# The lower part of the query times the upper part of the key, as two 64-row matmuls in two halves of the array

## Chip, cores and metric

The kernel runs on one core of a Trainium2 chip. The metric is the device time of one execution in microseconds (us). TensorE is called PE in the profile, its weight loads PEld, VectorE is DVE, ScalarE is ACT, GpSimd is POOL, and SP is the engine whose queue issues the DMAs here.

## The reference

One layer of a decoder: a normed input is projected to queries, keys and values of 8 heads of 64 and to a gated short convolution; then an output projection and a SwiGLU feed-forward part. The change lies in the attention scores, the line with `z` below.

```python
def one_block(args):                      # 128 queries of every head
    z = jnp.einsum('bhqd,bhkd->bhqk', q_blk, k32) * scale
    causal = key_pos[None, :] < q_pos[:, None]
    sp = jax.nn.softplus(z)
    neg_log_rem = jnp.where(causal, sp, 0.0)
    after = lax.cumsum(neg_log_rem, axis=3, reverse=True) - neg_log_rem
    a = jnp.where(causal, jnp.exp((z - sp) - after), 0.0)
    return jnp.einsum('bhqk,bhkd->bhqd', a, v32)
```

The sequence has 2048 tokens, so a head has 16 query blocks (t = 0 to 15) of 128 and, for block t, t + 1 key blocks of 128.

## The kernel before, in words

Numbers are kept as a rounded upper part and the rest as a lower part, both in the type fp32r. The program has an opening (projection to q, k, v), the attention stage with the convolution's projections woven in, the output projection and the feed-forward part. The attention stage loops over 4 pairs of heads; in a pair it runs 48 units, 24 for each head. A unit is one query block t against up to 8 key blocks (`SB`), that is up to 1024 keys, and these fill one or two PSUM banks of 512 columns. A head has 16 units with two banks: 10 with 8 key blocks and 2 each with 7, 6 and 5; so all 8 heads have 128, with a second bank of 512 columns in 80, of 384 in 16, of 256 in 16 and of 128 in 16.

`scores` computes a unit on PE. In `k_st` the upper part of 64 key rows lies on partitions 0 to 63 and the lower part on 64 to 127. `q_hh` holds the upper part of the query on both halves, `q_ll` the lower part on both. So one matmul over 128 rows gives upper query times (upper + lower key) (line 1347), and a second gives lower query times (upper + lower key) (line 1348). A unit on the diagonal adds the causal mask by a bf16 matmul with the identity (line 1351). The last matmul of a unit raises `z_full`; then ACT makes two sigmoids of the scores (lines 1107, 1109), DVE scans their running product (line 1210, `scan_done`) and POOL multiplies (line 1269, `a_done`). `scores` of unit n waits for the scan of unit n-2, since `z` has two buffers.

The order on PE is written out by hand in `body`: scores of unit n, then a number of steps of the convolution's projection (`project_step`, lines 107 to 109, counts in the table `plan`), the transposes of unit n-3 (line 1363) and, at the end of a group, the products with the values (lines 1369, 1370). Each matmul is preceded by its own weight load, which overlaps matmuls before it.

The keys come in by `load_k` (line 959) and `load_k_rest` (line 965), on SP's queue. It is also this queue that issues the loads of the queries (line 976), of the projection's inputs `hT` (line 991) and weights (line 997), of the values (line 981) and the stores.

Of the kernel before, what the change touches and what calls it, by code (L numbers as in the profile page):

```python
# [20 lines left out]
F32 = mybir.dt.float32  # L21
# [6 lines left out]
P = 128  # L28
BANK = 512
EPS = 1e-6  # L30
MASKED = -1e30
DMA = 16


def wait(eng, sem, value):

    if not isinstance(value, int) or value > 0:
        eng.wait_ge(sem, value)
# [166 lines left out]
def whole_layer(nc, cst, x, norm_mix, w_in, q_norm, k_norm, conv_w, w_out, norm_ffn, w_gate, w_up, w_down, out, HD,  # L205
                hT_hi_dram, hT_lo_dram, qk_hi_dram, qk_lo_dram, v_dram, mixT_dram, wt_dram, x2_dram, h2_dram, ops_dram):

    with ExitStack() as stack:
# [40 lines left out]
        opening = qkv_stage(nc, stack, cst, qkv, ps, x, norm_mix, w_in, q_norm, k_norm, w_down, hT_hi_dram, hT_lo_dram,  # L249
                            qk_hi_dram, qk_lo_dram, v_dram, wt_dram)  # L250
        att_stage = attend_conv_stage(nc, stack, cst, att, ps, opening, hT_hi_dram, hT_lo_dram, w_in, conv_w, qk_hi_dram,
                                      qk_lo_dram, v_dram, mixT_dram, HD)

# [576 lines left out]
def attend_conv_stage(nc, stack, cst, sb, ps, opening, hT_hi_dram, hT_lo_dram, w_in, conv_w, qk_hi_dram, qk_lo_dram, v_dram,  # L830
                      mixT_dram, HD):

    D, S = hT_hi_dram.shape
# [9 lines left out]
    QB = 4  # L843
# [5 lines left out]
    CT = CD // P  # L849
    NPROJ = 3 * CT  # L850
    HALO = TAPS - 1
    COL0 = w_in.shape[1] - 3 * CD
    assert S // BANK == PAIRS and NG % QB == 0

# [4 lines left out]
    for gi, (h, g) in enumerate(groups):  # L859
        for i in range(GT):  # L860
            t = GT * g + i
# [49 lines left out]
    def is_first(p):  # L911

        return isinstance(p, int) and p == 0
# [5 lines left out]
    with ExitStack():  # L919
        m = Pool_(nc, stack, "att_")  # L920
        k_st, q_hh, q_ll, v_st, stick, a, aT_hi, aT_lo, o_low, o_sb, hT_hi, hT_lo, w_stage, w_hi, w_lo = (
            sb[n] for n in ("k_st", "q_hh", "q_ll", "v_st", "stick", "a", "aT_hi", "aT_lo", "o_low", "o_sb",
                            "hT_hi", "hT_lo", "w_stage", "w_hi", "w_lo"))
        taps, halo, c_sb, cu, conv, tapped, y = (
            sb[n] for n in ("taps", "halo", "c_sb", "cu", "conv", "tapped", "y"))
        z = [ps[:, 4 * i:4 * i + 2, :].rearrange("p b c -> p (b c)") for i in range(2)]
        tr = ps[:, 2:4, :].rearrange("p b (j t) -> p b j t", t=P)
        o, proj = ps[:, 7, :], ps[:, 6, :]
        TILES, SAFE = opening.tiles, opening.tiles - 3

        k_in, v_in = [m.sem("k_in0"), m.sem("k_in1")], [m.sem("v_in0"), m.sem("v_in1")]
# [21 lines left out]
        def sync(sp, mix):  # L953
            def load_k(p, h):
                wait(sp, z_full, NU * (p - 1) + head_end[h])
                rows = bass.ds((2 * p + h) * HD + AD, HD)
                keys = slice(0, SAFE * P if is_first(p) and h == 0 else S)
                for half, src in enumerate((qk_hi_dram, qk_lo_dram)):
                    sp.dma_start(k_st[half * HD:(half + 1) * HD, h, keys].bitcast(F32),
                                 src[rows, keys]).then_inc(k_in[h], DMA)  # L960

            def load_k_rest():

                for half, src in enumerate((qk_hi_dram, qk_lo_dram)):
                    sp.dma_start(k_st[half * HD:(half + 1) * HD, 0, SAFE * P:S].bitcast(F32),
                                 src[AD:AD + HD, SAFE * P:S]).then_inc(k_rest, DMA)

            def load_q(p, gi):
# [25 lines left out]
            def load_w(p, k):  # L994
                wait(sp, w_lo_done, NPROJ * p + k - 1)
                col = COL0 + (1, 2, 0)[k % 3] * CD + (k // 3) * P
                sp.dma_start(w_stage[:, k % 2, :, :], w_in.rearrange("(k p) f -> p k f", p=P)
# [22 lines left out]
            def load_ahead(sp):  # L1020

                load_w(0, 0)
                load_w(0, 1)
                sp.wait_ge(opening.qkT_stored[0], 2 * DMA * (SAFE // 2 + 1))
                sp.wait_ge(opening.qkT_stored[1], 2 * DMA * (SAFE // 2))
                sp.wait_ge(opening.xn_done, TILES)
                sp.wait_ge(opening.ss_done, TILES)
                load_k(0, 0)
                for gi in range(QB):
                    load_q(0, gi)  # L1030
# [9 lines left out]
            def start_up():  # L1040
                for b in range(2):
                    sp.wait_ge(opening.v_stored[b], DMA * TILES // 2)
                    sp.wait_ge(opening.qkT_stored[b], DMA * TILES)
                    sp.wait_ge(opening.hT_stored[b], DMA * TILES)
                load_v(0, 0)
                load_k_rest()
# [3 lines left out]
            def body(p):  # L1050
                if is_first(p):
                    start_up()
                for n, (gi, h, t, j0, nb) in enumerate(units):
# [11 lines left out]
                    if n == 9:  # L1065
                        load_k(p, 1)
# [15 lines left out]
                    if not is_last(p):  # L1082
                        if n == head_end[0] + 2:
                            load_k(p + 1, 0)
                        if n == head_end[0] + LAG + 3:
                            load_v(p + 1, 0)
                        for i in plan.reloads.get(n, ()):
                            load_hT(p + 1, i)
# [12 lines left out]
        def scalar(act, mix):  # L1101
# [27 lines left out]
            def take(p, k):  # L1129
                c = k // 3  # L1130
                if k % 3 == 1:
                    wait(act, conv_done, CT * p + c)
                    wait(act, halo_moved, 2 * (CT * p + c))
                    if is_first(p) and c == 0:
                        act.wait_ge(edges_set, 2)
                    nc.scalar.activation(cu[:, 0:HALO], halo[:, c, :], ACT.Copy).then_inc(halo_moved, 1)
                act.wait_ge(proj_full, NPROJ * p + k + 1)
# [7 lines left out]
                elif k % 3 == 1:  # L1145
                    nc.scalar.activation(cu[:, HALO:HALO + BANK], proj, ACT.Copy).then_inc(proj_out, 1)
                else:
                    wait(act, y_stored, DMA * (CT * p + c))
                    nc.scalar.activation(y[:, :], proj, ACT.Copy).then_inc(proj_out, 1)
                    act.wait_ge(cu_done, CT * p + c + 1)  # L1150
                    nc.scalar.activation(halo[:, c, :], cu[:, BANK:BANK + HALO], ACT.Copy).then_inc(halo_moved, 1)

# [110 lines left out]
        def gpsimd(pool, mix):  # L1263
# [8 lines left out]
            def c_times_u(p, c):  # L1272
                pool.wait_ge(proj_out, NPROJ * p + 3 * c + 2)
                nc.gpsimd.tensor_tensor(cu[:, HALO:HALO + BANK], cu[:, HALO:HALO + BANK], c_sb[:, :],
                                        ALU.mult).then_inc(cu_done, 1)
# [53 lines left out]
        def tensor(pe, mix):  # L1329
            def scores(p, n):  # L1330
                gi, h, t, j0, nb = units[n]
                if opens[n]:
                    if gi % HG == 0:
                        pe.wait_ge(k_in[h], 2 * DMA * p + 2 * DMA)
                    pe.wait_ge(q_in[gi % QB], 4 * DMA * (NG // QB) * p + 4 * DMA * (gi // QB + 1))
                if is_first(p) and h == 0 and t == SAFE:
                    pe.wait_ge(k_rest, 2 * DMA)
                if is_first(p) and n == 1:
                    pe.wait_ge(opening.qk_n_done, 2 * TILES)
                    pe.wait_ge(opening.v_done, TILES)  # L1340
                wait(pe, scan_done, NU * p + n - 1)
                tile = slice((t % GT) * P, (t % GT + 1) * P)
                for b0 in range(0, nb * P, BANK):
                    b1 = min(nb * P, b0 + BANK)
                    diagonal = j0 + b1 // P == t + 1
                    out, keys = z[n % 2][:, b0:b1], slice(j0 * P + b0, j0 * P + b1)
                    nc.tensor.matmul(out, q_hh[:, gi % QB, tile], k_st[:, h, keys], start=True, stop=False)  # L1347
                    last = nc.tensor.matmul(out, q_ll[:, gi % QB, tile], k_st[:, h, keys],  # L1348
                                            start=False, stop=not diagonal)
                    if diagonal:  # L1350
                        last = nc.tensor.matmul(z[n % 2][:, b1 - P:b1], cst["ident_bf"][:, :], cst["mask_bf"][:, :],  # L1351
                                                start=False, stop=True)
                last.then_inc(z_full, 1)

            def transposes(p, n):
# [60 lines left out]
            def body(p):  # L1416
                for n in range(NU):
                    scores(p, n)
                    if is_first(p) and n == 0:
                        rest(0)  # L1420
                        rest(1)
                    for k, i in plan.steps[n]:
                        project_step(p, k, i)
                    q, b = at(p, n - LAG)
                    closes = opens[b] and (n > LAG or not is_first(p))
                    if closes:
                        upper_values(q, units[b][0] - 1)
                    if n >= LAG or not is_first(p):
                        transposes(p, n - LAG)
                    if closes:  # L1430
                        lower_values(q, units[b][0] - 1)
                    for k, i in plan.held[n]:
                        project_step(p, k, i)
# [14 lines left out]
        p, half = PAIRS - 1, DMA * NG // 2  # L1448
# [1200 lines left out]
```

## Time and profile before

| what | value |
|---|---|
| median of 3 runs | 2471.56 us (2466.45 to 2473.23) |
| the profiled execution's own time | 2467.11 us |
| its span, first to last instruction | 2465.3 us |
| PE busy in the span | 2423.8 us, 98%, 12008 matmuls |
| weight loads busy | 2023.1 us, 82% |
| DVE, ACT, POOL busy | 59%, 47%, 50% |
| chain of work that ended last | 92% on PE |

Busy time of an engine is the time in which at least one of its instructions runs. Matmuls overlap: one of 512 columns is shown with some 390 ns, while the next begins 0.23 us after it. So a matmul's cost to the program is read from the distance between two starts in the timeline, not from its own length.

### The profile page before, as it was taken

The page shows a single profiled execution, that of the slowest core. Times are in us where ns is not written, and L with a number is a line of the kernel's source. Part 1 is how long each engine was busy: PE and PEld are TensorE (multiplying, and loading weights), DVE is VectorE, ACT ScalarE, POOL GpSimd, SP SyncE. Part 2 cuts the span into 40 slices and gives each one's busy share as a digit, 9 for nine tenths or more (in the row PEclk, how much of TensorE's full clock was granted, in tenths as well). Part 3 has the DMA queues.
Part 4 walks back from the last instruction along what each step waited for, and adds up shares of the span by engine and source line. Part 5 has one row for each costly group of instructions (what it writes and reads, how often), then busy time and mean ns, then how long its engine had stood idle before and what let it go on. Part 6 is the DMA issues. An engine that isn't in the chain of part 4 may idle for free.

```text
span 2465.3 us, 34564 instructions
## 1 busy us (share of the span) xinstructions
PE 2423.8 (98%) x12008; PEld 2023.1 (82%) x12008; DVE 1456.8 (59%) x1499; ACT 1167.8 (47%) x1866; POOL 1238.5 (50%) x882
## 2 busy tenths in 40 slices
PE   8999999999999999999999999999999999999999
PEld 6888878888888888888788888878878888888887
DVE  4444367787677777536665555456646555554554
ACT  4322267777777777423533333334533333333333
POOL 1455366878777777204654545305856545450021
PEclk9999999999999999999999999999999999999999
DMA  6989864443534632444333232486642332325665
GB/s 196 319 285 291 255 183 122 140 114 100 164 95 114 175 112 75 153 135 164 124 115 111 87 122 82 144 269 232 226 165 80 112 128 77 115 94 184 222 216 201
DMA packets 337513, 388.15 MB, mean 157 GB/s; under 512 B 21473, under 2 KB 242785, under 8 KB 335073
## 3 DMA queue, kind: packets, MB, share of 16 engines
q1 hardware_dynamic: 337376, 386.49, 49.7%
q8 instruction: 67, 1.10, 0.2%
q14 instruction: 70, 0.57, 0.1%
HBM read 263.20 MB, written 123.21 MB: 157 GB/s over the span
## 4 chain that ended last, share of the span: by engine, by line
PE 92%; DVE 2%; DMA 2%; issue 1%; ACT 1%; POOL 1%; SPq 0%; ACTq 0%; DVEq 0%; POOLq 0%
PE lay_ps L2549 11%; PE lay_ps L2551 11%; PE lay_ps L2553 11%; PE lay_ps L107 9%; PE lay_ps L108 9%; PE lay_ps L109 9%; PE lay_ps L2579 5%; PE lay_ps L2581 5%; PE lay_ps L2580 5%; PE lay_ps L1363 5%; PE lay_ps L1347 3%; PE lay_ps L1348 3%; PE lay_ps L1370 3%; PE lay_ps L1369 2%; DMA lay_A_over<-in_w_down 1%
## 5 line engine op out<-in xcount | busy, mean ns | idle before, releaser
L2453 POOL TENSOR_TENSOR lay_A<-lay_raw,lay_A 128x512 fp32r<-128x512 f32 x264 | 364.9, 1394 | 384.9 <-ACT lay_A L2079 384.9
L2549 PE MATMUL lay_ps<-lay_B,lay_A 128*128 128x512 f32 x1232 | 481.0, 390 | 3.6 <-ACT lay_s L2101 3.6
L2551 PE MATMUL lay_ps<-lay_B,lay_A 128*128 128x512 f32 x1232 | 480.7, 390 | 0.0
L2553 PE MATMUL lay_ps<-lay_B,lay_A 128*128 128x512 f32 x1232 | 480.6, 390 | 0.0
L1210 DVE TENSOR_TENSOR_SCAN lay_stick<-lay_ps,lay_stick 128x128 f32<-128x128 f32 (+5 forms) x192 | 331.1, 1725 | 140.4 <-ACT lay_ps L1109 138.3
L1269 POOL TENSOR_TENSOR lay_a<-lay_a,lay_stick 128x128 f32<-128x128 f32 (+5 forms) x192 | 281.6, 1473 | 120.5 <-DVE lay_stick L1210 107.9
L2326 DVE TENSOR_TENSOR lay_A<-lay_A_over,lay_A 128x1024 fp32r<-128x1024 f32 x154 | 212.6, 1383 | 173.7 <-ACT lay_A L2123 173.1
L2079 ACT ACTIVATE lay_A<-lay_raw 128x512 fp32r<-128x512 f32 x264 | 162.1, 627 | 298.3 <-DMA lay_raw<-in_w_gate 124.5
L2123 ACT ACTIVATE lay_A<-lay_A_over 128x1024 fp32r<-128x1024 f32 x154 | 163.1, 1060 | 243.6 <-PE lay_ps L2581 201.2
L2549 PEld LDWEIGHTS lay_ps<-lay_B,lay_A 128*128 128x128 f32 x1232 | 232.0, 188 | 52.7 <-issue 2.6
L2553 PEld LDWEIGHTS lay_ps<-lay_B,lay_A 128*128 128x128 f32 x1232 | 232.0, 188 | 48.4
L2551 PEld LDWEIGHTS lay_ps<-lay_B,lay_A 128*128 128x128 f32 x1232 | 232.0, 188 | 48.0
L2579 PE MATMUL lay_ps<-lay_A 128*128 128x512 f32 x616 | 240.6, 391 | 3.9 <-ACT lay_s L2134 1.4
L2580 PE MATMUL lay_ps<-lay_A 128*128 128x512 f32 x616 | 239.7, 389 | 0.0
L2581 PE MATMUL lay_ps<-lay_A 128*128 128x512 f32 x616 | 239.7, 389 | 0.0
L1222 DVE TENSOR_TENSOR lay_aT_lo<-lay_ps,lay_aT_hi 128x512 fp32r<-128x512 f32 (+2 forms) x320 | 179.7, 594 | 24.7 <-ACT lay_aT_hi L1120 24.2
L1120 ACT ACTIVATE lay_aT_hi<-lay_ps 128x512 fp32r<-128x512 f32 (+2 forms) x320 | 156.2, 532 | 50.6 <-PE lay_ps L1363 50.3
L1107 ACT ACTIVATE lay_a<-lay_ps 128x128 f32<-128x128 f32 (+5 forms) x192 | 149.5, 779 | 64.7 <-PE lay_ps L1351 35.9
L107 PE MATMUL lay_ps<-lay_hT_hi,lay_w_hi 128*128 128x512 f32 x384 | 164.9, 429 | 3.2 <-issue 3.2
L2296 DVE TENSOR_TENSOR lay_s<-lay_ps,lay_s 128x512 f32<-128x512 f32 x132 | 90.2, 688 | 130.6 <-PE lay_ps L2553 92.9
L1363 PE MATMUL lay_ps<-all_ident,lay_a 128*128 128x128 f32 x1088 | 153.1, 275 | 6.3 <-DVE lay_aT_lo L1222 5.9
L2101 ACT ACTIVATE lay_s<-lay_ps 128x512 f32<-128x512 f32 x132 | 78.1, 592 | 166.2 <-PE lay_ps L2553 163.4
(148 smaller groups left out, 4954.4 us busy)
## 6 DMA issues: line engine op xcount, KB each, us to landing
hid_ops<-lay_s SPq DMA_DIRECT2D x154, 256.0 KB, 2.1
lay_A_over<-hid_ops SPq DMA_DIRECT2D x154, 256.0 KB, 2.8
lay_w_stage<-in_w_in SPq DMA_DIRECT2D x48, 512.0 KB, 4.7
lay_raw<-in_w_gate SPq DMA_DIRECT2D x22, 1024.0 KB, 5.7
lay_raw<-in_w_up SPq DMA_DIRECT2D x22, 1024.0 KB, 8.1
lay_A_over<-wd_ops SPq DMA_DIRECT2D x88, 256.0 KB, 3.0
lay_A_over<-in_w_down SPq DMA_DIRECT2D x66, 256.0 KB, 4.5
lay_wd_raw<-in_w_down SPq DMA_DIRECT2D x11, 1024.0 KB, 6.7
```

What stands on the lines that cost most here:

```text
L107: nc.tensor.matmul(out, lhs_hi, rhs_hi, start=first, stop=False)
L108: nc.tensor.matmul(out, lhs_hi, rhs_lo, start=False, stop=False)
L1210: nc.vector.tensor_tensor_scan(stick[:, row % 2, c0:c1][:, ::-1], z[n % 2][:, 0:nb * P][:, ::-1], stick[:, row % 2, S:S + 1].to_broadcast( ...
L1269: nc.gpsimd.tensor_tensor(a[:, n % 4, 0:nb * P], a[:, n % 4, 0:nb * P], stick[:, row_of[n] % 2, c0:c0 + nb * P], ALU.mult).then_inc(a_done, 1)
L1363: last = nc.tensor.transpose(tr[:, f % 2, i, :], a[:, n % 4, (j + i) * P:(j + i + 1) * P], cst["ident"][:, :])
L2453: nc.gpsimd.tensor_tensor(A[:, j, p, 1, :, :], operand(j, p), A[:, j, p, 0, :, :].bitcast(F32), ALU.subtract).then_inc(lo_done, 1)
L2549: nc.tensor.matmul(ps[:, b, :], A[:, j, p, 0, k, :], B[p][:, 0, k, :], start=first_mm, stop=False, skip_group_check=True)
L2551: nc.tensor.matmul(ps[:, b, :], A[:, j, p, 0, k, :], B[p][:, 1, k, :], start=False, stop=False, skip_group_check=True)
L2553: mm = nc.tensor.matmul(ps[:, b, :], A[:, j, p, 1, k, :], B[p][:, 0, k, :], start=False, stop=last_mm, skip_group_check=True)
L2579: nc.tensor.matmul(to, hi_op[:, toks], hi_op[:, wd_part], start=first, stop=False, skip_group_check=True)
L2580: nc.tensor.matmul(to, hi_op[:, toks], lo_op[:, wd_part], start=False, stop=False, skip_group_check=True)
L2581: mm = nc.tensor.matmul(to, lo_op[:, toks], hi_op[:, wd_part], start=False, stop=c == ROUNDS - 1, skip_group_check=True)
```

## The change

In a unit with two banks the upper-query matmuls of both banks now come first. Then the lower-query matmuls follow, and each has only 64 rows: for the first bank rows 0 to 63, for the second rows 64 to 127. In every second block of 512 keys the upper part of the key lies on partitions 64 to 127 and the lower part on 0 to 63, so that each 64-row matmul reads the upper part of its keys. The product of lower query and lower key is left out in these units. Units with one bank keep the 128-row matmul. The mask comes after all of these. The two 64-row matmuls of a unit are built for an array of 64 by 128 at row 0 and at row 64; all others use the whole 128 by 128. The loads of the keys are cut at every 512 keys: 8 DMAs for a head where there were 2.

```diff
+    KEY_LOADS = 2 * S // BANK
...
-                keys = slice(0, SAFE * P if is_first(p) and h == 0 else S)
+                end = SAFE * P if is_first(p) and h == 0 else S
                 for half, src in enumerate((qk_hi_dram, qk_lo_dram)):
-                    sp.dma_start(k_st[half * HD:(half + 1) * HD, h, keys].bitcast(F32),
-                                 src[rows, keys]).then_inc(k_in[h], DMA)
+                    for b in range(0, S, BANK):
+                        place = (half + b // BANK) % 2 * HD
+                        keys = slice(b, min(b + BANK, end))
+                        sp.dma_start(k_st[place:place + HD, h, keys].bitcast(F32), src[rows, keys]).then_inc(k_in[h], DMA)
...
-                for b0 in range(0, nb * P, BANK):
+                banks = range(0, nb * P, BANK)
+                for b0 in banks:
                     b1 = min(nb * P, b0 + BANK)
-                    diagonal = j0 + b1 // P == t + 1
                     out, keys = z[n % 2][:, b0:b1], slice(j0 * P + b0, j0 * P + b1)
                     nc.tensor.matmul(out, q_hh[:, gi % QB, tile], k_st[:, h, keys], start=True, stop=False)
-                    last = nc.tensor.matmul(out, q_ll[:, gi % QB, tile], k_st[:, h, keys],
-                                            start=False, stop=not diagonal)
-                    if diagonal:
-                        last = nc.tensor.matmul(z[n % 2][:, b1 - P:b1], cst["ident_bf"][:, :], cst["mask_bf"][:, :],
-                                                start=False, stop=True)
+                diagonal = j0 + nb == t + 1
+                for b0 in banks:
+                    b1 = min(nb * P, b0 + BANK)
+                    out, keys = z[n % 2][:, b0:b1], slice(j0 * P + b0, j0 * P + b1)
+                    half = slice(0, P) if len(banks) == 1 else slice(HD * (b0 // BANK), HD * (b0 // BANK) + HD)
+                    last = nc.tensor.matmul(out, q_ll[half, gi % QB, tile], k_st[half, h, keys],
+                                            start=False, stop=not diagonal or b0 != banks[-1])
+                if diagonal:
+                    last = nc.tensor.matmul(z[n % 2][:, (nb - 1) * P:nb * P], cst["ident_bf"][:, :], cst["mask_bf"][:, :],
+                                            start=False, stop=True)
                 last.then_inc(z_full, 1)
```

The first place is on PE, in the first head pair: a unit with 7 key blocks (banks of 512 and 384 columns) and the projection steps behind it. The shapes are those of the outputs. Before:

```order
L1347 MATMUL lay_ps<-lay_k_st,lay_q_hh 128x512
L1348 MATMUL lay_ps<-lay_k_st,lay_q_ll 128x512
L1347 MATMUL lay_ps<-lay_k_st,lay_q_hh 128x384
L1348 MATMUL lay_ps<-lay_k_st,lay_q_ll 128x384
L1351 MATMUL lay_ps<-all_mask_bf,all_ident_bf 128x128
L107 MATMUL lay_ps<-lay_hT_hi,lay_w_hi 128x512
L108 MATMUL lay_ps<-lay_hT_lo,lay_w_hi 128x512
```

And with the change, at the same place:

```order
L1351 MATMUL lay_ps<-lay_k_st,lay_q_hh 128x512
L1351 MATMUL lay_ps<-lay_k_st,lay_q_hh 128x384
L1357 MATMUL lay_ps<-lay_k_st,lay_q_ll 128x512
L1357 MATMUL lay_ps<-lay_k_st,lay_q_ll 128x384
L1360 MATMUL lay_ps<-all_mask_bf,all_ident_bf 128x128
L107 MATMUL lay_ps<-lay_hT_hi,lay_w_hi 128x512
L108 MATMUL lay_ps<-lay_hT_lo,lay_w_hi 128x512
```

The number of matmuls is the same; the two with `q_ll` now stand side by side, and the array changes from 128 rows to 64 ahead of the first of them and back behind the second.

The second place is on SP's queue near the end of the opening, where the first keys and queries are loaded. Before:

```order
L997 DMA lay_w_stage<-in_w_in 128x8x128 x2
L959 DMA lay_k_st<-qk_hi 64x1664
L959 DMA lay_k_st<-qk_lo 64x1664
L976 DMA lay_q_hh<-qk_hi 64x256
L976 DMA lay_q_ll<-qk_lo 64x256
```

With the change:

```order
L1001 DMA lay_w_stage<-in_w_in 128x8x128 x2
L963 DMA lay_k_st<-qk_hi 64x512 x3
L963 DMA lay_k_st<-qk_hi 64x128
L963 DMA lay_k_st<-qk_lo 64x512 x3
L963 DMA lay_k_st<-qk_lo 64x128
L980 DMA lay_q_hh<-qk_hi 64x256
L980 DMA lay_q_ll<-qk_lo 64x256
```

The loads of the queries and all that SP issues behind them now stand behind 8 issues for keys, not 2.

## Rows read from the trace of the kernel before

**Rows 1.** The page's first part: busy time, share of the span.

```profile
span 2465.3 us, 34564 instructions
...
PE 2423.8 (98%) x12008; PEld 2023.1 (82%) x12008; DVE 1456.8 (59%) x1499; ACT 1167.8 (47%) x1866; POOL 1238.5 (50%) x882
```

**Rows 2.** Attention stage: length, busy PE, PEld, DVE, ACT, POOL; clock, DMA.

```profile
340.00:640.00 300.00, 298.93 (x1856) 256.01 (x1855) 229.89 (x257) 232.65 (x399) 229.62 (x156) 1.00 0.42 113
```

**Rows 3.** Waits of PE from 300 to 990 us, the largest: total, times, longest.

```profile
PE lay_ps L1363 <- DVE lay_aT_lo L1222: 5.9, 6, 1.2
```

**Rows 4.** Timeline of PE, a unit with 512 and 512 columns: start, length.

```profile
607.11 0.39 PE L1348 MATMUL lay_ps<-lay_k_st,lay_q_ll 128*128 128x512 f32 x1
607.33 0.39 PE L1347 MATMUL lay_ps<-lay_k_st,lay_q_hh 128*128 128x512 f32 x1
607.57 0.39 PE L1348 MATMUL lay_ps<-lay_k_st,lay_q_ll 128*128 128x512 f32 x1
607.80 0.39 PE L107 MATMUL lay_ps<-lay_hT_hi,lay_w_hi 128*128 128x512 f32 x1
```

**Rows 5.** Timeline of PE, end of a unit with 512 and 384 columns.

```profile
540.76 0.34 PE L1348 MATMUL lay_ps<-lay_k_st,lay_q_ll 128*128 128x384 f32 x1
540.94 0.23 PE L1351 MATMUL lay_ps<-all_mask_bf,all_ident_bf 128*128 128x128 bf16 x1
540.98 0.48 PE L107 MATMUL lay_ps<-lay_hT_hi,lay_w_hi 128*128 128x512 f32 x1
541.29 0.40 PE L108 MATMUL lay_ps<-lay_hT_lo,lay_w_hi 128*128 128x512 f32 x1
```

**Rows 6.** Groups of PE by form: the lower-query matmuls of all units; busy, mean ns.

```profile
L1348 PE MATMUL lay_ps<-lay_k_st,lay_q_ll 128*128 128x512 f32 x224 | 89.0, 397 | 0.0
...
L1348 PE MATMUL lay_ps<-lay_k_st,lay_q_ll 128*128 128x384 f32 x32 | 10.8, 337 | 0.0
...
L1348 PE MATMUL lay_ps<-lay_k_st,lay_q_ll 128*128 128x256 f32 x32 | 8.9, 279 | 0.0
L1348 PE MATMUL lay_ps<-lay_k_st,lay_q_ll 128*128 128x128 f32 x32 | 8.8, 275 | 0.0
```

**Rows 7.** Timeline of PE, second bank of 256 columns.

```profile
612.43 0.28 PE L1348 MATMUL lay_ps<-lay_k_st,lay_q_ll 128*128 128x256 f32 x1
612.55 0.23 PE L1351 MATMUL lay_ps<-all_mask_bf,all_ident_bf 128*128 128x128 bf16 x1
```

**Rows 8.** Timeline of PE, second bank of 128 columns.

```profile
604.37 0.27 PE L1348 MATMUL lay_ps<-lay_k_st,lay_q_ll 128*128 128x128 f32 x1
604.48 0.23 PE L1351 MATMUL lay_ps<-all_mask_bf,all_ident_bf 128*128 128x128 bf16 x1
```

**Rows 9.** Timeline of the weight loads, the mask's; idle before it in brackets.

```profile
540.93 0.10 PEld L1351 LDWEIGHTS lay_ps<-all_mask_bf,all_ident_bf 128*128 128x128 bf16 x1 [0.16 <-issue]
```

**Rows 10.** Timeline of PE, start after a pause.

```profile
309.88 0.47 PE L107 MATMUL lay_ps<-lay_hT_hi,lay_w_hi 128*128 128x512 f32 x1 [3.25 <-issue]
310.19 0.39 PE L108 MATMUL lay_ps<-lay_hT_lo,lay_w_hi 128*128 128x512 f32 x1
...
310.66 0.55 PE L107 MATMUL lay_ps<-lay_hT_hi,lay_w_hi 128*128 128x512 f32 x1
```

**Rows 11.** Timeline of SP's queue near the end of the opening.

```profile
274.64 0.59 SPq L959 DMA_DIRECT2D lay_k_st<-qk_lo  x1
275.27 0.60 SPq L976 DMA_DIRECT2D lay_q_hh<-qk_hi  x1
...
298.53 0.48 SPq L991 DMA_DIRECT2D lay_hT_lo<-hT_lo  x1
```

**Rows 12.** DMA issues from 240 to 340 us: count, size, median us to landing.

```profile
lay_hT_lo<-hT_lo SPq DMA_DIRECT2D x8, 256.0 KB, 7.6
```

**Rows 13.** Timelines of DVE and PE: a scan, and the scores that wait for it.

```profile
569.91 2.35 DVE L1210 TENSOR_TENSOR_SCAN lay_stick<-lay_ps,lay_stick 128x1024 f32<-128x1024 f32 x1 [1.42 <-ACT lay_ps L1109]
...
572.80 0.47 PE L1347 MATMUL lay_ps<-lay_k_st,lay_q_hh 128*128 128x512 f32 x1
```

More of the change, by code:

```diff
@@ L956, in load_k @@
                 rows = bass.ds((2 * p + h) * HD + AD, HD)
-                keys = slice(0, SAFE * P if is_first(p) and h == 0 else S)
+                end = SAFE * P if is_first(p) and h == 0 else S
                 for half, src in enumerate((qk_hi_dram, qk_lo_dram)):
-                    sp.dma_start(k_st[half * HD:(half + 1) * HD, h, keys].bitcast(F32),
-                                 src[rows, keys]).then_inc(k_in[h], DMA)
+                    for b in range(0, S, BANK):
+                        place = (half + b // BANK) % 2 * HD
+                        keys = slice(b, min(b + BANK, end))
+                        sp.dma_start(k_st[place:place + HD, h, keys].bitcast(F32), src[rows, keys]).then_inc(k_in[h], DMA)
             def load_k_rest():
                 for half, src in enumerate((qk_hi_dram, qk_lo_dram)):
-                    sp.dma_start(k_st[half * HD:(half + 1) * HD, 0, SAFE * P:S].bitcast(F32),
+                    place = (half + 1) % 2 * HD
+                    sp.dma_start(k_st[place:place + HD, 0, SAFE * P:S].bitcast(F32),
                                  src[AD:AD + HD, SAFE * P:S]).then_inc(k_rest, DMA)
@@ L1333, in scores @@
                     if gi % HG == 0:
-                        pe.wait_ge(k_in[h], 2 * DMA * p + 2 * DMA)
+                        pe.wait_ge(k_in[h], KEY_LOADS * DMA * p + KEY_LOADS * DMA)
                     pe.wait_ge(q_in[gi % QB], 4 * DMA * (NG // QB) * p + 4 * DMA * (gi // QB + 1))
```

## The prediction

> **What bounds the kernel now.** I read the page's busy times first: PE works 98% of the span, no other engine over 59% [rows 1]. An average over stages proves little, so I took the attention stage alone: in 300 us of it PE is busy 298.93 us, DVE, ACT and POOL some 230 us each, at the full clock [rows 2]. Then the waits: from 300 to 990 us PE's largest wait in total is 5.9 us in 6 times [rows 3]. So in this stage time is PE time, and what PE gains or loses is gained or lost in full as long as the others keep up. As busy time counts overlapping matmuls, I price everything by distances between starts.
>
> **What the change saves at best.** In the timeline a lower-query matmul of 512 columns is followed by the next start after 0.23 us [rows 4], one of 384 after 0.18 [rows 5], one of 256 after 0.12 [rows 7], one of 128 after 0.11 [rows 8]. If the two 64-row matmuls of a unit run side by side, the second bank's one costs nothing any more. There are 80 second banks of 512 columns and 16 each of 384, 256 and 128; the counts agree with the groups, 224 being 128 first banks, 16 single banks and these 80, and 32 being 16 and 16 [rows 6]. The saving is 80 x 0.23 + 16 x (0.18 + 0.12 + 0.11) = 18.4 + 6.6 = 25.0 us, 0.195 us a unit.
>
> No row shows two matmuls side by side, so this needs bounds. Below, in series, the saving is nothing, as the columns stay as many. Between lies a pair whose second weight load can't begin before the first matmul starts; a 128-column matmul, which is too short to cover a load, is followed after 0.11 us [rows 8], so the second would start 0.11 us later and about 0.12 us a unit be left, 15.4 us. I take the full 25.0, because the loads go to different halves and 0.23 us of an upper-query matmul has room for two of 0.11.
>
> **What it costs.** Each of the 128 units changes the division of the array twice: from 128 rows to two times 64 and back. No row has such a change; these are the bounds.
> - Nothing, if it goes along with the data. The nearest row is the step from the last f32 matmul to the mask in bf16: it starts 0.18 us after a matmul of 384 columns, the ordinary distance [rows 5].
> - 0.08 us, if only the weights can't be loaded ahead. At the mask that is what happens: its weight load sat 0.16 us idle and began when the mask itself did [rows 9], and the projection behind it took 0.31 us to the next start and not 0.23 [rows 5].
> - 0.16 us, if the array must be empty. A matmul is shown with 0.39 us and the next starts after 0.23 [rows 4], so 0.16 us of every matmul lies behind the start of the next; that is what a new division would wait for.
> - 0.24 us, if it is empty and the weights come after that: 0.16 plus the 0.08 us which the first matmul after a pause takes more, 0.31 and not 0.23 [rows 10].
>
> I take 0.16 us. [...] The cost is 2 x 128 x 0.16 = 41.0 us.
>
> The Trainium skill speaks to both halves of this. TensorEngine Tiling (Array Packing), Key Properties, says that different tiles can load weights and multiply in parallel, and that changing the tiling mode drains the engine. TensorE: Matmul & The Clock Gate, Part 3, has matmuls on different row groups start some 4 ns apart. Neither gives the price of the drain, and no row here shows one; by the first rule alone the sum would be 25.0 us less, by the second 41.0 more.
>
> **What costs nothing.** The order of the matmuls: `z_full` rises with the last one as before, and the mask comes behind either way. The scans: DVE's row which PE follows most closely ends at 572.26 us and PE starts the scores at 572.80 [rows 13]; the unit between has one bank, so nothing in that distance changes; elsewhere a unit loses or gains 0.3 us at most against more room. Were a saving of PE to meet a late scan, it would be cut there, not turned into a loss.
>
> SP's queue: 6 more issues at each load of keys. At the first, near the opening's end, a key load took 0.63 us from its start to the next issue [rows 11], so all behind it may come 3.8 us later. What is due next is `hT`: the lower part of its second tile is issued at 298.53 us [rows 11], lands 7.6 us later by the median [rows 12], at 306.1, and PE takes that tile at 310.66 [rows 10]. That leaves 4.5 us, so 3.8 is covered; without that cover it would be at most 3.8 us, once. The other seven loads of keys are issued about 15 units ahead of their use and the query loads behind them two groups ahead; 3.8 us is hidden there. The bytes are the same.
>
> **The sum.** The profiled execution took 2467.1 us. 2467.1 - 25.0 + 41.0 = 2483.1 us. The median of the three runs stands 4.4 us above the profiled execution, within their spread; I keep to the profiled one. A difference under 0.3%, 7.4 us, a measurement of this kernel can't tell from none.
>
> **The rivals.**
> 1. The array changes its division without a stop, and the halves run side by side. For it: the mask's ordinary distance [rows 5]. Against: the mask changes no rows. 2467.1 - 25.0 = 2442.1 us, or 2451.7 where the second weight load comes late. It decides where a change costs less than 25.0 / 256 = 0.098 us; below 0.069 us it would be told from no change.
> 2. Only the weight loads are exposed, 0.08 us at each change, 20.5 us. For it: the mask again [rows 9]. 2462.6 us, no change to be told. This case covers changes of 0.069 to 0.127 us.
> 3. Full stops with weights after them, 0.24 us each: 61.4 - 25.0 = 36.4 us more, 2503.5 us. Stops of 0.16 us and the two halves in series, where the change doesn't do what it says, come out alike, 2508.1 us. For it: the first matmul after a pause [rows 10]. Against: the trace loads weights one matmul ahead nearly everywhere.
>
> **How the numbers follow.** Forecast, changes of about 0.16 us, 0.32, own range 2475 to 2495. Rival 1, 0.31, over 2442 to 2459; rival 2, 0.20; rival 3, 0.17. The forecast is hardly likelier than rival 1, but it lies with rival 3 on the slower side, which together holds 0.49. Faster 0.31, same 0.20, slower 0.49. The range leaves out the lowest tenth of rival 1 and the upper end of rival 3: 2443 to 2508.
>
> **What would show it.** In the changed timeline: the distance from the first `q_ll` matmul of a pair to the second, near 0 side by side, 0.11 with late weights, 0.23 in series. The distance from the last `q_hh` start to the first `q_ll` start, 0.23 us for 512 columns without a stop, 0.39 with my price. The same from the second `q_ll` to the projection behind it. The weight loads of `q_ll`: ahead of their matmuls or with them. PE's waits for `hT` and scans should stay. I am wrong if the distance from the first `q_hh` of a 512 and 512 unit to the matmul behind the unit, 0.92 us in four ordinary steps, falls under 0.87, or if it goes past 1.15.

## The result, and the profile of the changed kernel

The changed kernel takes 2486.78 us (median of 4 runs, 2485.15 to 2489.36). The kernel before, measured beside it, takes 2469.91 us (4 runs, 2466.45 to 2473.23). The ratio is 1.0071, with a 95% interval of 1.0055 to 1.0087: slower by 16.9 us. The profiled execution took 2485.15 us.

The page's first part, busy time of each engine, against [rows 1]:

```profile
span 2483.4 us, 34648 instructions
PE 2438.3 (98%) x12008; PEld 1991.5 (80%) x12008; DVE 1460.9 (59%) x1499; ACT 1167.7 (47%) x1866; POOL 1240.3 (50%) x882
```

The span is 18.1 us longer than that of [rows 1]. PE is busy 14.5 us more, although the number of matmuls is the same; DVE, ACT and POOL moved by no more than 4.1 us, and the weight loads are busy 31.6 us less. The attention stage is still PE's alone; this is the view by windows, with the columns of [rows 2]:

```profile
340.00:640.00 300.00, 299.10 (x1806) 236.73 (x1805) 226.11 (x253) 227.56 (x392) 225.90 (x153) 1.00 0.41 115
```

In the same 300 us PE gets through 1806 matmuls and not 1856, with as little idle time. So PE isn't waiting for other engines; its matmuls stand farther apart. PE's waits from 300 to 990 us confirm it. First the next two rows of the kernel before, behind the one in [rows 3]:

```profile
PE lay_ps L1347 <- DVE lay_stick L1210: 3.9, 2, 3.2
PE lay_ps L107 <- issue: 3.2, 1, 3.2
```

and the three with the change:

```profile
PE lay_ps L1372 <- DVE lay_aT_lo L1226: 5.9, 5, 2.5
PE lay_ps L1351 <- DVE lay_stick L1214: 3.8, 2, 3.1
PE lay_ps L107 <- issue: 3.3, 1, 3.3
```

Now the place itself: the timeline of PE for a unit with two banks of 512 columns and no mask, where a projection step comes ahead and behind; to be set against [rows 4].

```profile
550.53 0.63 PE L1351 MATMUL lay_ps<-lay_k_st,lay_q_hh 128*128 128x512 f32 x2
551.08 0.50 PE L1357 MATMUL lay_ps<-lay_k_st,lay_q_ll 64*128 64x512 f32 x2
551.52 0.50 PE L107 MATMUL lay_ps<-lay_hT_hi,lay_w_hi 128*128 128x512 f32 x1
551.86 0.39 PE L108 MATMUL lay_ps<-lay_hT_lo,lay_w_hi 128*128 128x512 f32 x1
```

Read it by starts. A row with x2 holds two like matmuls. The `q_ll` pair lasts 0.50 us as a whole, which is the length of one (501 ns by the groups below), so the two cover the same stretch; their records start 3 ns apart. The second bank's matmul is free, as hoped. But three steps are longer than 0.23 us. From 550.53 to the pair it is 0.55 us for two steps, and 0.46 would be ordinary: 0.09 more. From the pair to L107 it is 0.44, 0.21 more. And from L107 to L108, where both have 128 rows, it is 0.34, 0.11 more. All three together cost 0.41 us, and the free matmul gave 0.23.

The timeline of the weight loads shows what else happens at the same place (in brackets: idle before, counterpart of [rows 9]):

```profile
551.08 0.19 PEld L1357 LDWEIGHTS lay_ps<-lay_k_st,lay_q_ll 64*128 64x128 f32 x2 [0.36 <-issue]
551.52 0.19 PEld L107 LDWEIGHTS lay_ps<-lay_hT_hi,lay_w_hi 128*128 128x128 f32 x1 [0.25 <-issue]
551.62 0.19 PEld L108 LDWEIGHTS lay_ps<-lay_hT_lo,lay_w_hi 128*128 128x128 f32 x1
551.86 0.19 PEld L109 LDWEIGHTS lay_ps<-lay_hT_hi,lay_w_lo 128*128 128x128 f32 x1
```

L109's weights are loaded at 551.86 for a matmul at 552.09: one matmul ahead, as nearly everywhere. (The matmul at 552.09 is the row of the timeline behind the last one shown.) The weights of the pair and of L107 are not: each load begins with its own matmul, at 551.08 and 551.52, after 0.36 and 0.25 us without any load. So it is in all 128 units of this trace: the loads of the pair, and of the matmul behind it, begin within 5 ns of their matmuls.

Where the mask follows the pair, one of the three steps is missing. PE's timeline of a unit with banks of 512 and 384 columns, against [rows 5]:

```profile
546.41 0.65 PE L1351 MATMUL lay_ps<-lay_k_st,lay_q_hh 128*128 128x512 f32 x2
546.99 0.49 PE L1357 MATMUL lay_ps<-lay_k_st,lay_q_ll 64*128 64x512 f32 x2
547.41 0.23 PE L1360 MATMUL lay_ps<-all_mask_bf,all_ident_bf 128*128 128x128 bf16 x1
547.45 0.48 PE L107 MATMUL lay_ps<-lay_hT_hi,lay_w_hi 128*128 128x512 f32 x1
547.77 0.40 PE L108 MATMUL lay_ps<-lay_hT_lo,lay_w_hi 128*128 128x512 f32 x1
```

From L107 to L108 it is 0.32 us here and was 0.31 in [rows 5]: behind a mask that step was long already, so the change adds nothing to it.

The 64-row matmuls in the groups of PE by form, for [rows 6]; 208 are 128 first banks and 80 second ones:

```profile
L1357 PE MATMUL lay_ps<-lay_k_st,lay_q_ll 64*128 64x512 f32 x208 | 64.3, 501 | 0.0
L1357 PE MATMUL lay_ps<-lay_k_st,lay_q_ll 64*128 64x384 f32 x16 | 7.0, 440 | 0.0
L1357 PE MATMUL lay_ps<-lay_k_st,lay_q_ll 64*128 64x256 f32 x16 | 6.1, 379 | 0.0
L1357 PE MATMUL lay_ps<-lay_k_st,lay_q_ll 64*128 64x128 f32 x16 | 5.2, 325 | 0.0
```

From the starts of all units in both traces, first `q_hh` to the third start behind the scores, the median differences are:

| second bank | units | longer by, us each | in all, us |
|---|---|---|---|
| 512 columns, no mask | 64 | 0.161 | 10.3 |
| 512 columns, mask | 16 | 0.058 | 0.9 |
| 384 columns, mask | 16 | 0.102 | 1.6 |
| 256 columns, mask | 16 | 0.167 | 2.7 |
| 128 columns, mask | 16 | 0.179 | 2.9 |

That makes 18.4 us, against the 18.1 us of the span. No kind of two-bank unit gains; those with one bank stay as they were.

### The profile page after: what moved, and what is told of

Its sections match the earlier page's. It is cut to its first block, busy times and chain, and to the rows that moved or that the text cites. A ratio compares the mean times of both kernels' runs of the same rounds, so it can differ in the third digit from the quotient of the medians.

```text
span 2483.4 us, 34648 instructions
## 1 busy us (share of the span) xinstructions
PE 2438.3 (98%) x12008; PEld 1991.5 (80%) x12008; DVE 1460.9 (59%) x1499; ACT 1167.7 (47%) x1866; POOL 1240.3 (50%) x882
## 4 chain that ended last, share of the span: by engine, by line
PE 91%; DVE 2%; DMA 2%; SPq 1%; issue 1%; ACT 1%; POOL 1%; ACTq 0%; DVEq 0%; POOLq 0%
PE lay_ps L2558 11%; PE lay_ps L2562 11%; PE lay_ps L2560 11%; PE lay_ps L107 10%; PE lay_ps L108 9%; PE lay_ps L109 9%; PE lay_ps L2588 5%; PE lay_ps L2590 5%; PE lay_ps L2589 5%; PE lay_ps L1372 5%; PE lay_ps L1378 3%; PE lay_ps L1379 3%; PE lay_ps L1351 2%; PE lay_ps L1357 2%; PE lay_ps L1360 1%
## 5 line engine op out<-in xcount | busy, mean ns | idle before, releaser
L107 PE MATMUL lay_ps<-lay_hT_hi,lay_w_hi 128*128 128x512 f32 x384 | 170.3, 444 | 3.3 <-issue 3.3
```

The costliest lines, as they stand in the source:

```text
L107: nc.tensor.matmul(out, lhs_hi, rhs_hi, start=first, stop=False)
```

## The experiments

Ratios are to the kernel before, on the same chip, with 95% intervals. "Theory" in the expectations is that the change of division costs the time.

**Same order and loads, no 64-row matmuls.** The lower-query matmuls keep 128 rows; the product of the two lower parts is computed again.

```diff
-                    half = slice(0, P) if len(banks) == 1 else slice(HD * (b0 // BANK), HD * (b0 // BANK) + HD)
+                    half = slice(0, P)
```

> The changed kernel with its loads of the keys, its swapped halves and its order (both upper-query matmuls, then both lower-query ones), but every lower-query matmul over all 128 rows. Theory (the price is the change of the array's division): back to the kernel before, ratio 1.000, within 0.0015, and every step in the timeline of scores at its ordinary distance. Rival (the order of the matmuls or the 8 loads instead of 2 cost it): ratio 1.004 to 1.007, near the changed kernel.

Measured: 2470.99 us, ratio 1.0014 (1.0005 to 1.0023). PE's timeline of the same unit as at 550.53 above:

```profile
544.54 0.63 PE L1351 MATMUL lay_ps<-lay_k_st,lay_q_hh 128*128 128x512 f32 x2
545.01 0.62 PE L1357 MATMUL lay_ps<-lay_k_st,lay_q_ll 128*128 128x512 f32 x2
545.47 0.40 PE L107 MATMUL lay_ps<-lay_hT_hi,lay_w_hi 128*128 128x512 f32 x1
545.71 0.39 PE L108 MATMUL lay_ps<-lay_hT_lo,lay_w_hi 128*128 128x512 f32 x1
```

All steps are 0.23 us again: 0.47, 0.46, 0.24. The long steps belong to the 64-row matmuls, not to the order. A rest of 0.14% stays, whose interval doesn't reach down to no change.

**Both 64-row matmuls in the same half.** The keys stay unswapped, and both matmuls use rows 0 to 63.

```diff
-                        place = (half + b // BANK) % 2 * HD
+                        place = half * HD
...
-                    place = (half + 1) % 2 * HD
+                    place = half * HD
...
-                    half = slice(0, P) if len(banks) == 1 else slice(HD * (b0 // BANK), HD * (b0 // BANK) + HD)
+                    half = slice(0, P) if len(banks) == 1 else slice(0, HD)
```

> Both lower-query matmuls of a two-bank unit over rows 0 to 63, keys not swapped, so that they share a half of the array; two changes of division a unit as in the changed kernel. Theory (the halves run side by side, 0.003 us apart): the second bank's 25.0 us come back, 2486.8 + 25.0 = 2511.8 us, ratio 1.017, the second matmul of a pair 0.23 us behind the first. Rival (the 0.003 us is only how the starts are recorded, and the pair takes the time of two): ratio 1.007, as the changed kernel.

Measured: 2509.44 us, 1.0168 (1.0153 to 1.0183). PE's timeline of the same unit:

```profile
557.24 0.63 PE L1351 MATMUL lay_ps<-lay_k_st,lay_q_hh 128*128 128x512 f32 x2
557.80 0.73 PE L1357 MATMUL lay_ps<-lay_k_st,lay_q_ll 64*128 64x512 f32 x2
558.46 0.50 PE L107 MATMUL lay_ps<-lay_hT_hi,lay_w_hi 128*128 128x512 f32 x1
558.80 0.40 PE L108 MATMUL lay_ps<-lay_hT_lo,lay_w_hi 128*128 128x512 f32 x1
```

From the pair's start to L107 it is now 0.66 us and not 0.44. Side by side is worth 0.0097 of the time, 24 us; the units' starts in the two traces give 24.1. This case also parts the two steps that the pair hides. By the records, which the row with x2 merges, `q_ll` to `q_ll` takes 0.34, where the expectation had 0.23, and the second one to L107 0.32. So behind a change the first step costs 0.11 more, and the step into the next change 0.09 more.

**Four changes a unit and not two.** Each bank's `q_hh` and 64-row `q_ll` alternate; nothing runs side by side.

```diff
-                for b0 in banks:
-                    b1 = min(nb * P, b0 + BANK)
-                    out, keys = z[n % 2][:, b0:b1], slice(j0 * P + b0, j0 * P + b1)
-                    nc.tensor.matmul(out, q_hh[:, gi % QB, tile], k_st[:, h, keys], start=True, stop=False)
...
+                    nc.tensor.matmul(out, q_hh[:, gi % QB, tile], k_st[:, h, keys], start=True, stop=False)
                     last = nc.tensor.matmul(out, q_ll[half, gi % QB, tile], k_st[half, h, keys],
```

> The 64-row matmuls apart: upper query, lower query (rows 0 to 63), upper query, lower query (rows 64 to 127), so four changes of division a unit and nothing side by side. Theory (each visit to 64 rows costs about 0.39 us more than the matmul's own columns, 0.29 where the mask comes behind it): 64 units x 0.80 + 64 units x 0.69 = 95 us, about 2563 us, ratio 1.038. Rival (empty array only, weights loaded ahead, 0.16 us a change as the prediction took it): 4 x 128 x 0.16 = 82 us, 2550 us, ratio 1.033. Rival (64-row matmuls are slow in themselves, 0.2 us each, and the change costs nothing): 2 x 128 x 0.2 = 51 us, ratio 1.021.

Measured: 2557.97 us, 1.0363 (1.0348 to 1.0379), between the theory's number and that of the first rival. PE's timeline of the same unit decides:

```profile
574.93 0.39 PE L1353 MATMUL lay_ps<-lay_k_st,lay_q_hh 128*128 128x512 f32 x1
575.25 0.49 PE L1354 MATMUL lay_ps<-lay_k_st,lay_q_ll 64*128 64x512 f32 x1
575.67 0.50 PE L1353 MATMUL lay_ps<-lay_k_st,lay_q_hh 128*128 128x512 f32 x1
576.10 0.50 PE L1354 MATMUL lay_ps<-lay_k_st,lay_q_ll 64*128 64x512 f32 x1
576.53 0.49 PE L107 MATMUL lay_ps<-lay_hT_hi,lay_w_hi 128*128 128x512 f32 x1
576.86 0.40 PE L108 MATMUL lay_ps<-lay_hT_lo,lay_w_hi 128*128 128x512 f32 x1
```

The steps are 0.32, 0.42, 0.43, 0.43, 0.33. The first has only the part ahead of a change (0.09), the last only the part behind one (0.10), and those between have both (0.19 to 0.20). The total came out at 89 us, under the theory's 95, which had already spared the units with a mask the last part: these are 0.63 to 0.68 us longer where it had 0.69, the others 0.78 where it had 0.80. The middle steps are longer by 0.19 to 0.20 us with every width of the second bank.

**The pair first.** `q_ll` of both banks, then `q_hh` of both.

```diff
-                    nc.tensor.matmul(out, q_hh[:, gi % QB, tile], k_st[:, h, keys], start=True, stop=False)
+                    half = slice(0, P) if len(banks) == 1 else slice(HD * (b0 // BANK), HD * (b0 // BANK) + HD)
+                    nc.tensor.matmul(out, q_ll[half, gi % QB, tile], k_st[half, h, keys], start=True, stop=False)
...
-                    last = nc.tensor.matmul(out, q_ll[half, gi % QB, tile], k_st[half, h, keys],
+                    last = nc.tensor.matmul(out, q_hh[:, gi % QB, tile], k_st[:, h, keys],
```

> The pair of 64-row matmuls first in the unit, the upper-query ones behind it. Theory (a change costs an emptying of about 0.1 us and a weight load of 0.11 us that can't run ahead; where the weights already come late, behind transposes or ahead of the mask, the second part is not paid again): units without a mask gain 0.08 us against the changed kernel, since the entry lies behind transposes; units with a mask lose about 0.03, since the mask no longer hides the exit's weights. 64 x 0.08 - 64 x 0.03 = 3 us less, 2483 us, ratio 1.0055 to 1.006. Rival (only the emptying costs): no difference from the changed kernel in any unit, ratio 1.007.

Measured: 2493.94 us, 1.0110 (1.0093 to 1.0126). Both expectations missed. PE's timeline at the unit with 512 and 384 columns, which has transposes ahead of it:

```profile
547.63 0.66 PE L1372 MATMUL lay_ps<-all_ident,lay_a 128*128 128x128 f32 x4
548.23 0.50 PE L1353 MATMUL lay_ps<-lay_k_st,lay_q_ll 64*128 64x512 f32 x2
548.65 0.68 PE L1357 MATMUL lay_ps<-lay_k_st,lay_q_hh 128*128 128x512 f32 x2
549.17 0.23 PE L1360 MATMUL lay_ps<-all_mask_bf,all_ident_bf 128*128 128x128 bf16 x1
```

And its weight loads:

```profile
548.22 0.19 PEld L1353 LDWEIGHTS lay_ps<-lay_k_st,lay_q_ll 64*128 64x128 f32 x2 [0.17 <-issue]
548.65 0.30 PEld L1357 LDWEIGHTS lay_ps<-lay_k_st,lay_q_hh 128*128 128x128 f32 x2 [0.24 <-issue]
```

Behind the last transpose a 128-row matmul starts after 28 ns; the pair starts after 203 ns (both from the records, as the rows count four transposes as one). That step is longer by 0.175 us. I had thought that it was late anyway and would hide a part of the change. But a part of the 0.175 was paid before too, one step later; this is the kernel before at the same unit, behind transposes:

```profile
540.03 0.48 PE L1347 MATMUL lay_ps<-lay_k_st,lay_q_hh 128*128 128x512 f32 x1
540.35 0.40 PE L1348 MATMUL lay_ps<-lay_k_st,lay_q_ll 128*128 128x512 f32 x1
```

There `q_hh` comes early and the next start 0.32 us after it, not 0.23. So over the whole unit, from the start ahead of it to the third start behind it, transposes ahead change the price by 10 ns at most: with the pair first, units without a mask are 0.164 us longer than in the kernel before where they stand behind transposes, and 0.154 where they stand behind a projection step; in the changed kernel it is 0.163 and 0.156. What the order loses is the mask's cover of 0.11 us, which no longer stands next to the pair: units with a mask lose 0.04 to 0.11 us more than in the changed kernel, 6.1 us in all, and the two profiled executions differ by 7.0. So the changed kernel's order is the better of the two.

**The loads alone.** The kernel before, with each load of keys cut into 8 DMAs as in the change, halves not swapped, the computation as before.

```diff
+                    for b in range(0, S, BANK):
+                        place = half * HD
+                        keys = slice(b, min(b + BANK, end))
+                        sp.dma_start(k_st[place:place + HD, h, keys].bitcast(F32), src[rows, keys]).then_inc(k_in[h], DMA)
```

> The kernel before with nothing changed but the loads of the keys, 8 DMAs of 512 keys instead of 2, halves not swapped. If the loads are what the run with 128 rows everywhere lost (3 us), ratio 1.001 to 1.002, with the scores of some head late or one wait of PE longer. If they are hidden, as the prediction said, ratio 1.000, within 0.001.

Measured: 2470.47 us, 1.0020 (1.0011 to 1.0029), 3.9 us.

**The order alone.** The kernel before, with the `q_hh` of both banks ahead of the 128-row `q_ll`.

```diff
                     nc.tensor.matmul(out, q_hh[:, gi % QB, tile], k_st[:, h, keys], start=True, stop=False)
+                diagonal = j0 + nb == t + 1
+                for b0 in banks:
+                    b1 = min(nb * P, b0 + BANK)
+                    out, keys = z[n % 2][:, b0:b1], slice(j0 * P + b0, j0 * P + b1)
```

> The kernel before with nothing changed but the order on PE: both upper-query matmuls, both lower-query ones over 128 rows, then the mask; loads as before. If the order is what the run with 128 rows everywhere lost, ratio 1.001 to 1.002. If order costs nothing, as the prediction said, ratio 1.000, within 0.001.

Measured: 2468.33 us, 1.0004 (0.9995 to 1.0013). The order costs nothing that can be told; so what the run with 128 rows everywhere lost is put down to the loads.

**The pair twice.** The changed kernel, with the pair of `q_ll` made twice in a visit, so that the lower product is added twice.

```diff
+                for b0 in banks if len(banks) == 2 else ():
+                    b1 = min(nb * P, b0 + BANK)
+                    out, keys = z[n % 2][:, b0:b1], slice(j0 * P + b0, j0 * P + b1)
+                    half = slice(HD * (b0 // BANK), HD * (b0 // BANK) + HD)
+                    nc.tensor.matmul(out, q_ll[half, gi % QB, tile], k_st[half, h, keys], start=False, stop=False)
```

> The changed kernel with the pair of 64-row matmuls made twice in each visit to 64 rows, so that the lower product is added twice. Theory (the price is at the two changes alone, and inside a visit pairs follow each other with weights loaded ahead): 0.21 to 0.23 us a unit more, 27 to 30 us, 2514 to 2517 us, ratio 1.018 to 1.019. Rival (each 64-row pair pays for an emptied array and its weights by itself): 0.43 us a unit, 55 us, 2542 us, ratio 1.029.

Measured: 2516.02 us, 1.0201 (1.0185 to 1.0217), 29 us above the changed kernel by the medians and 32 by the ratios. The time is the theory's, the ratio a little over its own, and both are far under the rival's. PE's timeline, a unit of 512 and 512 columns:

```profile
611.44 0.71 PE L1351 MATMUL lay_ps<-lay_k_st,lay_q_hh 128*128 128x512 f32 x2
612.08 0.50 PE L1357 MATMUL lay_ps<-lay_k_st,lay_q_ll 64*128 64x512 f32 x2
612.41 0.40 PE L1362 MATMUL lay_ps<-lay_k_st,lay_q_ll 64*128 64x512 f32 x2
612.74 0.50 PE L107 MATMUL lay_ps<-lay_hT_hi,lay_w_hi 128*128 128x512 f32 x1
613.08 0.39 PE L108 MATMUL lay_ps<-lay_hT_lo,lay_w_hi 128*128 128x512 f32 x1
```

Pair to L107 was 0.44; it is now 0.33 + 0.33. The second pair adds 0.22 us, the time of its columns, and no further price. So the price belongs to the two changes of a visit, not to the 64-row matmuls.

**The kernel before again, and half of the cuts.** Two runs to find where the loads' 0.2% lies: the kernel before unchanged, and with 4 DMAs a load of keys (the diff is against the run with 8).

> The kernel before, unchanged: a second profile of it and its spread. Both theories: 1.000 within 0.001. If ACT's pause where its loop over head pairs goes from the second to the third is again 3.8 us, as in the first profile of it, the longer pauses of 5.2 to 5.8 us in the changed kernels are theirs; if it is 5 us or more here too, the pause varies by itself and says nothing about the key loads.

```diff
-                    for b in range(0, S, BANK):
+                    for b in range(0, S, 2 * BANK):
...
-                        keys = slice(b, min(b + BANK, end))
+                        keys = slice(b, min(b + 2 * BANK, end))
```

> The kernel before with each load of keys issued as 4 DMAs instead of 2 (8 in the changed kernel, which cost 0.2% by themselves). If the loss grows with the number of issues: 2 of the 6 more, a third of 4 to 5 us, 1.5 us or 1.0006. If it sits in something that only pieces of 512 keys do: 1.000. If it is a step that any further issue sets off: 1.002.

Measured: the kernel before 2468.48 us, 1.0004 (0.9995 to 1.0013); with 4 DMAs 2468.83 us, 1.0006 (0.9997 to 1.0015). The second sits at the number for a loss that grows with the issues, but its interval doesn't exclude nothing. In the units' starts the trace with 8 DMAs loses 2.0 us against the second profile of the kernel before at one place, where the third head pair begins, and 0.2 us from there to the end of the stage; it comes to that place 2.4 us late, but so does the first profile of the kernel before, with 2.6. There ACT starts a unit late. Its row there, first in the kernel before as first profiled:

```profile
653.62 0.28 ACT L1107 ACTIVATE lay_a<-lay_ps 128x128 f32<-128x128 f32 x1 [3.81 <-PE lay_ps L1348]
```

in its second profile:

```profile
651.94 0.28 ACT L1107 ACTIVATE lay_a<-lay_ps 128x128 f32<-128x128 f32 x1 [4.71 <-issue]
```

and with 8 DMAs:

```profile
655.43 0.28 ACT L1111 ACTIVATE lay_a<-lay_ps 128x128 f32<-128x128 f32 x1 [5.83 <-issue]
```

Idle 3.81, 4.71 and 5.83 us; with the order alone, which costs nothing, it was 5.34. The pause varies in one and the same kernel by 0.9 us, and the units' starts at this place by about 1.5 us between its two profiles. So it can hold a part of the loads' 3.9 us, and how much stays open.

## Why the prediction was right, and where it wasn't

The forecast of 2483.1 us stands 3.7 us under the measured median and 2 us under the profiled execution. The sign held, and so did the two halves of the sum, side by side and a price for each change; how that price is made up did not. Step by step:

**PE bounds the stage: right.** Each edit to its matmuls showed in the time at about the size that their starts show, and its waits stayed at the same totals (5.9, 3.8 and 3.3 us, where they were 5.9, 3.9 and 3.2).

**The saving of 25.0 us: right to 1 us.** The pair starts 3 or 4 ns apart. Put into the same half it costs 24 us more. The missing microsecond is in the 16 second banks of 128 columns, where the sum read 0.11 us from [rows 8] and 0.06 is saved by the units' starts. With the order alone, by the records, a `q_ll` of 128 columns is followed by the mask after 0.06 us, so the 0.11 wasn't the price of its columns. The doubt about a late second weight load fell away: the two loads run together, 0.19 us for both.

**The order costs nothing: right,** 1.0004. The scans stayed too.

**The price of a change, 0.16 us: the size near, what it is made of wrong.** The run with both matmuls in the same half pays for the changes and saves nothing. It is 40.8 us above the kernel before by the medians and 42.5 by its units' starts, which is 0.160 to 0.166 us for each of 256 changes; the sum had 41.0. No row had decided between the four bounds, so 0.16 was a choice. But the step argued that only the array must be empty and that weights are still loaded ahead. That failed: the load begins with its matmul, the idle ahead of it is 0.36 and 0.25 us. What stands in its place has two parts. The step into the change costs 0.09 us, the step behind the first matmul after it 0.11. A full change is thus 0.20 us; a mask behind it hides the second part. In the prediction's own distances: from `q_hh` to the pair I gave 0.39 us and it is 0.33, by the records; from the pair to the projection I gave 0.39 and it is 0.44; and the 0.11 one step later I didn't foresee. Too much at the entry and too little at the exit nearly cancelled, and half of the units have a mask that hides a part, so the mean of 0.16 is luck: a visit costs some 0.40 us without a mask and 0.24 to 0.29 with one, where the sum had 0.32 for each. Rival 3 had the form of it, a stop with the weights after it, with 0.24 where 0.20 and, before a mask, 0.09 was paid. Rival 2's 0.08 is about one of the two parts. Rival 1 is out: the experiment with no change of division gave back the whole difference but 0.14%.

That 0.09 is the array running empty and 0.11 the weights' late load is argued from the loads' rows, not shown; no run has one without the other. What is shown is that both appear wherever the division changes, at every width: with four changes a unit they make 0.19 to 0.20 us together, and in the changed kernel the step from the last `q_hh` to the pair is longer by 0.087 to 0.095 us behind second banks of 512, 384, 256 and 128 columns. The Trainium skill's rule in TensorEngine Tiling (Array Packing), Key Properties, that a change of the tiling mode drains the engine and that different tiles load and multiply in parallel, agrees with the trace: a change costs 0.20 us, and the two halves start 3 ns apart. That the engine empties is what the Trainium skill says; the trace shows only what a change costs.

**The test of 0.92 us.** I named 0.87 and 1.15 as the bounds within which I was right. The distance is 0.99 us, and 0.11 us more one step on.

**SP's queue costs nothing: wrong, by 0.2%.** The cover at the start held as worked out. This is SP's queue in the changed kernel, the lower part of the second `hT` tile, which [rows 11] have at 298.53:

```profile
302.67 0.49 SPq L995 DMA_DIRECT2D lay_hT_lo<-hT_lo  x1
```

It is issued 4.1 us later, and PE still takes up the projections at the same time, behind the same pause as in [rows 10]:

```profile
309.98 0.47 PE L107 MATMUL lay_ps<-lay_hT_hi,lay_w_hi 128*128 128x512 f32 x1 [3.25 <-issue]
310.29 0.40 PE L108 MATMUL lay_ps<-lay_hT_lo,lay_w_hi 128*128 128x512 f32 x1
...
310.76 0.62 PE L107 MATMUL lay_ps<-lay_hT_hi,lay_w_hi 128*128 128x512 f32 x1
```

So the loss isn't where I had looked for one. Alone the cut loads cost 3.9 us, 2.4 with the order and without the 64-row matmuls. In the changed kernel's profile it can't be seen apart: the units' steps already make up the whole of the span's difference, and the interval of the ratio, 13.6 to 21.5 us, holds both the steps alone and the steps with 3 us more.

## What to carry to other kernels

Read a trade like this by visits, not by matmuls. A pair of 64-row matmuls of 512 columns saves 0.23 us, and going into the other division and back costs 0.40, or 0.29 where something that hides the second part already stands behind. One pair a visit therefore loses; from the second pair, whose saving comes without a further price, the sum turns to a gain of 0.06 us by these numbers, an estimate that no run here made. Let the pair stand just ahead of a step that is late anyway, such as the mask here: without that cover the kernel came out at 1.0110 and not at 1.0071. What stands ahead of the pair, transposes or a projection step, changed the price by 10 ns at most over the whole unit. And count a change of what a DMA is cut into as a change of its own: time it alone.

## What the runs showed of the hardware that was not expected

- The price of a changed division is paid in two places: 0.09 us at the step into it, 0.11 at the step after the first matmul, where nothing has changed any more. Whoever reads only the step at the change sees half.
- It doesn't depend on the columns of the matmul ahead: 0.087 to 0.095 us from 512 columns down to 128.
- Behind 128-column transposes the step into it is longer by 0.175 us and not 0.09. The difference was there without the change too, one step later, so over the unit it costs the same: 0.164 us behind transposes, 0.154 behind a projection step.
- Eight DMAs of 128 KB for a load of keys and not two of 512 KB cost 0.2% of a kernel (1.0011 to 1.0029) in which PE is busy 98% of the time and waits for none of them; four cost less than can be told. Where the time goes stays open.
